# Two weight loads of a mixture-of-experts encoder leave the wait for the first gather of token rows

## The reference

```python
def hier_moe(x, w_r1, b_r1, w_r2, b_r2, w_gate, w_up, w_down):
    logit1 = (xt @ w_r1) + b_r1                 # 4 groups
    grp = argmax(logit1); p_grp = max(softmax(logit1))
    logit2 = logits of the 8 experts of that group
    top_p, top_e = top_k(softmax(logit2), 2)
    gates = p_grp * top_p / sum(top_p)
    # for each block of rows that chose expert e:
    hidden = silu(xb @ w_gate[e]) * (xb @ w_up[e])
    y = sum over the two experts of gate * (hidden @ w_down[e])
for i in range(2):
    x = x + (pool_mix if i == 0 else band attention)(rms_norm(x))
    x = x + hier_moe(rms_norm(x))
```

## Time and profile before

| | |
|---|---|
| median of three executions | 1471.44 us |
| the profiled execution | 1471.15 us |
| its span (first to last record) | 1469.2 us |
| TensorE busy | 1286.6 us (88%) |
| VectorE, ScalarE, GpSimd busy | 344.4, 308.6, 233.3 us |
| moved in all | 477.39 MB, mean 325 GB/s |
| layer 0: first gather issued, last weight loads under way | 70 us, about 565 us |
| layer 1: first gather issued, last weight loads under way | 944 us, about 1432 us |

### The profile page before, as it was taken

How to read it: one execution, slowest core, us unless ns; L and a number is a source line. 1 busy time by engine, 2 the same in 40 slices (tenths; PEclk the granted TensorE clock), 3 DMA queues, 4 the chain that set the end, 5 groups by cost and what they waited for, 6 DMA issues and landing times. The chain is left out here.

```text
span 1469.2 us, 17145 instructions
## 1 busy us (share of the span) xinstructions
PE 1286.6 (88%) x6316; PEld 650.9 (44%) x6316; DVE 344.4 (23%) x719; ACT 308.6 (21%) x638; POOL 233.3 (16%) x391
## 2 busy tenths in 40 slices
PE   9999888888878889999998999999978887888782
PEld 7643333333333333678776544643333343333331
DVE  4621100000000003654317543611000000000003
ACT  4211111111111113343335432211111111111110
POOL 1111111111111102033232220111111111111100
PEclk9999999999999999999999999999998999999997
DMA  9799999999999998412047213999999999999995
GB/s 370 280 361 396 401 397 407 414 412 402 409 408 407 399 415 321 145 58 88 31 136 258 77 31 138 386 375 398 399 406 408 409 411 413 412 404 401 405 401 206
DMA packets 57484, 477.39 MB, mean 325 GB/s; under 512 B 11373, under 2 KB 12653, under 8 KB 31258
## 3 DMA queue, kind: packets, MB, share of 16 engines
q1 hardware_dynamic: 39134, 433.74, 73.5%
q0 software_dynamic: 15504, 33.98, 7.3%
q10 hardware_dynamic: 2796, 8.97, 1.7%
HBM read 464.34 MB, written 28.04 MB: 335 GB/s over the span
## 5 line engine op out<-in xcount | busy, mean ns | idle before, releaser
L1774 PE MATMUL ps<-ring,xT 128*64 128x512 f32 x352 | 182.2, 678 | 48.9 <-issue 40.5
L1444 DVE SCALAR_TENSOR_TENSOR nat<-nat,slot_gate,ps 64x512 f32<-64x512 f32 x64 | 47.3, 739 | 664.9 <-ACT nat L1004 664.7
L1774 PE MATMUL ps<-pair,xT 128*64 128x512 f32 x352 | 169.9, 640 | 37.2 <-DMA pair<-in_moe_w_up 37.2
L1774 PE MATMUL ps<-third_pair,xT 128*64 128x512 f32 x320 | 156.9, 648 | 45.5 <-issue 25.1
L1775 PE MATMUL ps<-ring,xT 128*64 128x512 f32 x352 | 182.6, 679 | 0.0
L707 POOL DMA_INDIRECT yb<-nat,scol x64 | 59.4, 928 | 775.0 <-DVE nat L1440 775.0
L1775 PE MATMUL ps<-pair,xT 128*64 128x512 f32 x352 | 170.4, 641 | 0.0
L1004 ACT ACTIVATE nat<-ps 64x512 f32<-64x512 f32 x64 | 38.0, 594 | 609.5 <-PE ps L1775 609.5
L1775 PE MATMUL ps<-third_pair,xT 128*64 128x512 f32 x320 | 157.3, 649 | 0.0
L1783 PE MATMUL ps<-qk,hidT 128*64 128x512 f32 x336 | 153.1, 598 | 1.2 <-ACT hidT L981 1.2
L1784 PE MATMUL ps<-qk,hidT 128*64 128x512 f32 x336 | 153.2, 598 | 0.0
(11 more groups left out here) (226 smaller groups left out, 1833.0 us busy)
## 6 DMA issues: line engine op xcount, KB each, us to landing
qk<-in_moe_w_down SPq DMA_DIRECT2D x42, 2048.0 KB, 40.1
ring<-in_moe_w_down SPq DMA_DIRECT2D x22, 2048.0 KB, 40.1
pair<-in_moe_w_gate SPq DMA_DIRECT2D x22, 2048.0 KB, 34.6
pair<-in_moe_w_up SPq DMA_DIRECT2D x22, 2048.0 KB, 39.1
ring<-in_moe_w_gate SPq DMA_DIRECT2D x20, 2048.0 KB, 34.4
ring<-in_moe_w_up SPq DMA_DIRECT2D x20, 2048.0 KB, 38.9
third_pair<-in_moe_w_gate SPq DMA_DIRECT2D x20, 2048.0 KB, 34.9
third_pair<-in_moe_w_up SPq DMA_DIRECT2D x20, 2048.0 KB, 39.4
```

The source lines that it names most:

```text
L1444: return V.scalar_tensor_tensor(out=hidden, in0=silu, scalar=slot_gate[:, bass.ds(j, 1)], in1=ps[0:BLK, GU_BANK, :], op0=ALU.mult, op1=ALU ...
L1774: mm(ps[BLK:P, GU_BANK, :], rows, gate[:, at], start=(k == 0), stop=(k == KT - 1))
```

## The change

Two waits on SP's list change their company. In layer 0 the load of the down matrix of expert 1 stood behind the wait for the first gather; it now stands right behind the waits for the transposed and stored rows, ahead of the wait for the logits. In layer 1 the load of the up matrix of expert 2 stood behind the wait for the first gather; it now follows the gate load of that expert at once. SP doesn't wait for the gather any more in either layer. No instruction is added or removed except that wait, and no other engine's list changes.

```diff
                     sp.wait_ge(hT_ps, NT)
                     sp.wait_ge(xn_stored[l], 16 * NT)
+                    load_down(l, 1, 1)
                 else:
...
                 sp.wait_ge(logit_ps, 2 * (l + 1))
                 load_gate(l, 2, 2)
-                if l == 0:
-                    load_up(l, 2, 2)
-                sp.wait_ge(gathered[l][0], 16)
-                if l == 0:
-                    load_down(l, 1, 1)
-                else:
-                    load_up(l, 2, 2)
+                load_up(l, 2, 2)
 
                 sp.wait_ge(half_gu_ps, l + 1)
```

## The result

The changed kernel is slower: 1481.25 us against 1471.44 (medians of 13 executions each), a ratio of 1.0058 with a 95% interval of 1.0042 to 1.0076, or 8.5 us (6.2 to 11.2). Executions of one kernel spread more than the first three suggested: 1468 to 1478 us before, 1477 to 1486 after. The prediction was 1474.9 with a range up to 1478.6: right in sign and in naming layer 1, too small in size, and wrong for layer 0, which was to cost nothing.

The account below looks back on a forecast made before the run. Weight transfers were taken to bound the expert blocks from each first reload on, which waits for TensorE's block 0. 1471.15 + 0 (layer 0) + 3.7 (layer 1: 2.3 gather, 1.4 clock) gave 1474.9 us, range 1470.9 to 1478.6.

Parts of the forecast that it names:

- What bounds the kernel: Both layers' expert blocks: weight transfers bind from first to last reload, so each layer's end moves with its first reload.
- The late loads: Ahead of both first reloads: the two moved loads are hidden already; moving them earlier only widens an idle.
- Rival D: Both layers: moved bytes are worth their time, 4.9 us gained per move, 1461.4 us; D and other gains 0.06.
- The gather in layer 1: Layer 1's first gather, slowed by weight traffic, lands at about 952.4; block 0 starts 2.3 us late (0 to 3.4).
- The clock in layer 1: First half of block 0's products in layer 1: TensorE's clock falls after the idle, losing 1.4 us (0 to 1.7).
- Layer 0: Layer 0's first gather lands by 75.1, ahead of TensorE's need at 75.78: cost 0, margin 0.7 us.
- The sum: Whole kernel: 1471.15 + 0 for layer 0 + 3.7 for layer 1 = 1474.85 us, say 1474.9.
- rival C: Both layers' gathers late, layer 0's too by 1 to 3.4 us with a clock fall: 1478.3 us, chance 0.17.

Follow-up runs that it names:

- layer 1 only: Kernel before, with only layer 1's wait for the gather taken out, so its up load of expert 2 goes early: 1.0037, 5.4 us over before.
- six fillers: Kernel before, with 6 instead of 8 filler products ahead of block 0's transposes in both layers: 0.9977, 3.4 us faster than before.
- layer 0 only: Changed kernel with layer 1's wait put back, so only layer 0's down load of expert 1 moves: 1.0008 against the kernel before.
- half early: Kernel before, with the first half (1 MB) of layer 1's up load of expert 2 issued early, behind the gate load: 1.0025.
- kernel of the waiting second gather: Changed kernel, but POOL issues expert 1's gather only when expert 0's has landed; one execution, landings after 6.4 and 8.6 us, no time given.

## Why the prediction was wrong

*What bounds the kernel*, first: right, as far as can be told. The stretches behind the first reloads stayed at 466.4 and 513.1 us, but single profiles scatter in them by 4 us, so that one to one is shown only by the times: 5.4 us for 5.55 in the seams (layer 1 only), -3.4 for -3.2 (six fillers), 1.2 for 3.15 within its interval (layer 0 only), and 3.7 for 1.2 at the edge of its interval (half early). The late loads were hidden: moving one to the other side of the reload cost 4.9 us, moving it ahead gained nothing. Rival D is out.

*The gather in layer 1*: the step that failed in size. I had its packets start 1.8 us from issue, advance beside the weights to 64%, and do what is left in under 1 us, so that it lands 7.9 us from issue and is 2.3 us late. It took 9.1 and was 3.4 us late, which was the upper bound. The traffic ended where I put it (950.9 + 2.1 for the later start, against a drop between 953 and 954). What was wrong is the time at both of its ends. Its packets start only 4.1 us from issue (950.7; 4.3 in the kernel of the waiting second gather), and it lands at 955.7, 2.2 to 2.7 us behind the weights, not 1.5. That it advances beside them was right, as the packets of that kernel show. In the earlier trace rows the gather of 944.47 already lands 2.6 us behind the end of the weights at 946; I used only its duration. The test with half the load, 6.8 us where this model says 5.1, confirms the error.

*The clock in layer 1*: right in kind, small in size. Forecast 1.4 us within 0 to 1.7; measured 1.7 in the first profile (seam 5.2 less 3.4 of idle), 2.1 in the second and with layer 1 only, and gone when fillers cover the idle.

*Layer 0*: the step that failed in kind. I had it land at 75.1 with 0.7 us of margin, since "nothing but these 1.3 us can be lost" beside the weights. It took 7.0 us instead of 3.6, and was 1.3 us late, with 1.7 us for the clock in three of four profiles: 1.5 to 3.1 us where I had 0. The 1.3 us of overlap were reckoned from the first movement of the gather's packets at 72.0, as if that start were fixed. In the changed kernel they start 3.0 us from issue, not 1.8. Heavy traffic lasted until about 3.7 us behind the issue (I had 3.1), and the gather landed 3.3 us behind it (I had 1.8). So the "Cost 0" of this layer is the term that failed.

*The sum*: rival C, both layers late, is what happened, with the fall of the clock in layer 0 in the second profile but not in the first. That its 1478.3 us agree with the first profiled execution (1477.91) is luck: C adds 3.7 us for layer 1 and 3.4 for layer 0, and the seams of that execution have 5.2 and 1.5. The median, 1481.25, lies above C's range. The seams give 6.6 and 8.4 us in the two profiles of the changed kernel; the two measurements 8.5 and 5.3 us. I gave C a chance of 0.17, because I judged the margin of layer 0 by a model of sharing, with a fixed start, that no row of before had shown.

## What to carry to other kernels

A wait ahead of a bulk load can be worth keeping for what it keeps out of the way: a small transfer on the critical path, issued while the bulk is in flight, landed here only when the bulk was through, with up to 7 us of it ahead, although in layer 1 its bytes had moved earlier. A load that lands in an idle of the transfer engines gains nothing from an earlier place; look for the event that ends this idle, here the first reload, and move that one, by as much as the late load leaves free. Fillers that keep TensorE's clock up should end where the awaited transfer lands: two too many cost 1.7 and 1.5 us in the two layers, and an idle of 3.4 us cost 1.7 to 2.1 us of clock on top.

## What the runs showed of the hardware that I had not expected

A gather of up to 64 rows of 4 KB, 3.4 to 3.6 us beside idle engines, takes 4.1, 7.0, 6.8, 7.8 and 9.1 us where heavy weight traffic lasts about 1.5, 3.7, 4.5, 5.4 and 6.9 us from its issue: it lands 2.2 to 3.3 us behind the end of that traffic each time. Yet in layer 1 its bytes move beside the weights, as the packets show; they start 4.1 to 4.3 us from issue instead of 1.7. In layer 0 they start 3.0 us from issue, just as the weights end. Where the traffic never ends a gather gets through in the midst of it, after 9.0 us. So the 9.1 us may be what any gather takes in heavy traffic, and not 6.9 of traffic and 2.2 more; no run with a longer traffic that ends tells the two apart.

The clock doesn't always fall behind the same idle. With TensorE idle for 1.34 us ahead of block 0 it stayed at 2.4 GHz in one profile of the changed kernel; with 1.33, 1.31 and 1.02 us it fell to 1.2 GHz for over 3 us in three others; with 1.20 us in layer 1 of the kernel with half a load early it did not, and behind the idles of 2.13, 2.97 and 3.4 us at these seams it fell each time. A second fall, in 15 to 25 us of the span, comes in some executions whatever the order of loads and costs 3 us or more; it is probably a good part of why executions of one kernel scatter. Of the seven profiled executions with it six lie 1.5 to 6.7 us above the median of their kernel, and of the five without it that have a median to compare with, four lie below theirs. The windows from 15 to 20 us of the kernel before and of the changed kernel (PE busy, granted clock, share, GB/s):

```profile
15.00:20.00 5.00, 5.00 (x34) 1.00 1.06 339
```

```profile
15.00:20.00 5.00, 5.00 (x23) 0.55 1.08 374
```
